# One TensorE program step for scores and PV, and ones columns of the values written by VectorE, in a dilated-attention layer on Trainium2

## The reference, cut to what matters

```
a = rms_norm(x);  [u_pool | q | k | v] = a @ w_in
mixer A: causal means over 2/4/8/16 tokens, minus the token, a 128x128 map per group, a scale
mixer B: 8 heads of 64, q and k normalised per head, T5 bias
  for (window, dilation) in ((128,1), (512,4), (2048,16)):
      blocks of 128 queries against 256 gathered keys (the block before, and the own one)
      p = exp(q k^T + bias), masked;  acc = p @ v;  l = sum(p)
  o = sum of the three acc / sum of the three l
h = x + concat(A, B) @ w_out
y = h + relu(rms_norm(h) @ w_up)^2 @ w_down
```

## Time and profile before

| what | value |
|---|---|
| time, two runs | 2589.89 and 2750.8 us, median 2670.34 us |
| the profiled execution's own time | 2590.12 us |
| its span on the slowest core (core 1) | 2588.6 us |
| spans of the 8 cores | 2569.7 to 2588.6 us |
| PE busy | 2098.6 us (81%) |
| ACT, DVE, POOL busy | 883.8, 850.9, 301.1 us |
| PE's share of the chain that ended last | 67% |

### The profile page before, as it was taken

How to read it: one execution, slowest core, us unless ns; L and a number is a source line. 1 busy time by engine, 2 the same in 40 slices (tenths; PEclk the granted TensorE clock), 3 DMA queues, 4 the chain that set the end, 5 groups by cost and what they waited for, 6 DMA issues and landing times.

```text
span 2588.6 us, 36200 instructions; the slowest of 8 cores (2569.7 to 2588.6 us)
## 1 busy us (share of the span) xinstructions
PE 2098.6 (81%) x11006; PEld 990.3 (38%) x11006; DVE 850.9 (33%) x1197; ACT 883.8 (34%) x1585; POOL 301.1 (12%) x277
## 2 busy tenths in 40 slices
PE   3466667999984999898995677899995989989897
PEld 1222223555541434343332233555552333434342
DVE  0324442444441313222221543344442322223120
ACT  1634615555541312121111454455552312212120
POOL 0001111333330000000000110333330000000000
PEclk8678979555657999999997799656566999999999
DMA  3699981000003646464545332000003445555454
GB/s 68 167 137 164 144 108 21 2 1 2 1 1 85 160 129 172 127 166 130 159 122 157 99 66 33 1 1 1 1 1 81 115 142 159 142 155 143 145 126 128
DMA packets 389896, 243.71 MB, mean 94 GB/s; under 512 B 275104, under 2 KB 368544, under 8 KB 389456
## 3 DMA queue, kind: packets, MB, share of 16 engines
q1 hardware_dynamic: 360080, 198.16, 28.1%
q0 software_dynamic: 29632, 43.24, 12.4%
HBM read 267.77 MB, written 33.60 MB: 116 GB/s over the span
## 4 chain that ended last, share of the span: by engine, by line
PE 67%; DMA 11%; ACT 6%; DVE 6%; issue 6%; POOL 2%; SPq 1%; ACTq 0%; DVEq 0%; POOLq 0%
PE ps L131 64%; ACT abf L139 5%; DMA af<-xc 4%; PE ps L135 3%; DVE af L143 3%; DMA abf<-w_in 2%; DMA abf<-wup_bf 2%; POOL abf L143 1%; DMA abf<-w_out 1%; DVE abf L147 1%; DVE abf L143 1%; ACT af L139 1%; DMA abf<-fd 1%; DMA abf<-xc 1%; SPq L159 1%
## 5 line engine op out<-in xcount | busy, mean ns | idle before, releaser
L131 PE MATMUL ps<-abf 128*128 128x512 bf16 (+2 forms) x4248 | 863.8, 360 | 113.6 <-POOL abf L143 40.8
L131 PE MATMUL ps<-abf,kv 128*128 128x512 bf16 (+1 forms) x3584 | 783.1, 359 | 66.6 <-DVE kv L143 14.5
L131 PEld LDWEIGHTS ps<-abf 128*128 128x128 bf16 (+1 forms) x4248 | 401.2, 111 | 570.0 <-issue 280.1
L139 ACT ACTIVATE abf<-ps 128x512 bf16<-128x512 f32 (+2 forms) x588 | 381.9, 669 | 475.8 <-PE ps L131 266.9
L131 PEld LDWEIGHTS ps<-abf,kv 128*128 128x128 bf16 (+1 forms) x3584 | 332.7, 111 | 437.7 <-issue 231.5
L139 ACT ACTIVATE af<-ps 128x512 f32<-128x512 f32 (+1 forms) x356 | 211.8, 595 | 604.7 <-PE ps L131 603.9
L143 DVE TENSOR_TENSOR kv<-af 128x512 bf16<-128x512 f32 x256 | 177.3, 693 | 303.6 <-ACT af L139 303.6
L143 POOL TENSOR_TENSOR abf<-abf,tabs 128x512 bf16<-128x512 bf16 x192 | 222.0, 1157 | 405.2 <-ACT abf L139 140.7
L131 PE MATMUL ps<-yaT,abf 128*128 128x512 bf16 x672 | 170.7, 406 | 26.5 <-DMA abf<-w_in 13.2
L143 DVE TENSOR_TENSOR abf<-abf,tabs 128x512 bf16<-128x512 bf16 x192 | 84.7, 441 | 308.4 <-ACT abf L139 255.0
L139 ACT ACTIVATE abf<-abf 128x512 f32<-128x512 f32 (+1 forms) x112 | 83.6, 750 | 248.9 <-DVE abf L143 149.0
(11 more groups left out here) (56 smaller groups left out, 888.6 us busy)
## 6 DMA issues: line engine op xcount, KB each, us to landing
abf<-wup_bf SPq DMA_DIRECT2D x256, 256.0 KB, 3.4
abf<-wdn_bf SPq DMA_DIRECT2D x256, 256.0 KB, 2.9
af<-xc SPq DMA_DIRECT2D x64, 512.0 KB, 4.5
abf<-w_in POOLq DMA_DIRECT2D x21, 1024.0 KB, 17.6
abf<-xc SPq DMA_DIRECT2D x16, 512.0 KB, 7.5
wup_bf<-w_up POOLq DMA_DIRECT2D x8, 1024.0 KB, 34.4
wdn_bf<-w_down POOLq DMA_DIRECT2D x8, 1024.0 KB, 39.6
out<-af SPq DMA_DIRECT2D x16, 512.0 KB, 4.7
```

Source lines behind the costliest of these rows:

```text
L131: return lambda e: e.matmul(out, lhsT=lhsT, rhs=rhs, start=start, stop=stop)
L139: return lambda e: e.activation(out=out, in_=in_, func=func, **kw)
```

## The change

Turn i of the loop makes one PE step out of scores(i) and pv(i - 2). The order of the instructions on PE stays: four score matmuls, then four PV matmuls. Their waits now all stand ahead of the first score matmul, and one semaphore increment, at the last PV matmul, stands for both. The steps after them (exp, mult, accumulation) are issued behind it in the order they had. Apart from that the ones columns of vp are written on DVE instead of POOL: a memset instead of the large copy, and the small copies as they were.

```diff
-            P.op("pool", CP(vp[e][:, :, oc:oc + 64], bass.AP(ones64[:].tensor, ones64[:].offset,
-                                                             [list(ones64[:].ap[0]), [0, NVT], [1, 64]])),
-                 reads=[R_const], writes=[R.vp1[e]])
+            P.op("dve", lambda e_, dst=vp[e][:, :, oc:oc + 64]: e_.memset(dst, 1.0), reads=[R_const], writes=[R.vp1[e]])
             if c == 1:
...
-                    P.op("pool", CP(dst, srcb), reads=[R_const], writes=[R.vp1[e]])
+                    P.op("dve", CP(dst, srcb), reads=[R_const], writes=[R.vp1[e]])
...
-        def scores(item):
+        def scores_prep(item):
...
-            P.op("pe", grp(fns), reads=[R_q, R_kv[0], R_kv[1]], writes=[R_bank[sbk]])
             pi = cn["p"] % 3
             cn["p"] += 1
...
+            def post():
+                P.op("act", ACT(PTr[pi], S, AF.Exp), reads=[R_bank[sbk]], writes=[R.PTr[pi]])
+                P.op(eng, TT(PT[pi].rearrange("p (a b) -> p a b", a=2), PTr[pi].rearrange("p (a b) -> p a b", a=2), tab_b, ALU.mult),
+                     reads=[R.PTr[pi], R_tabs], writes=[R.PT[pi]])
+            return (fns, [R_q, R_kv[0], R_kv[1]], [R_bank[sbk]]), post, pi
...
-            P.op("pe", grp(fns), reads=[R.vp[e], R.vp1[e], R.PT[pi]], writes=[R_bank[ob]])
...
+            return (fns, [R.vp[e], R.vp1[e], R.PT[pi]], [R_bank[ob]]), post
...
+            parts, posts = [], []
             if i < NP:
-                pis[i] = scores(pairs[i])
+                part, post, pis[i] = scores_prep(pairs[i])
+                parts.append(part)
+                posts.append(post)
             if i - LOOK >= 0:
-                pv(pairs[i - LOOK], pis.pop(i - LOOK))
+                part, post = pv_prep(pairs[i - LOOK], pis.pop(i - LOOK))
+                parts.append(part)
+                posts.append(post)
+            P.op("pe", grp([f for it in parts for f in it[0]]), reads=[r for it in parts for r in it[1]],
+                 writes=[w for it in parts for w in it[2]])
+            for post in posts:
+                post()
```

More of the change, by code:

```diff
@@ L749, in scores, with pv_prep @@
                     fns.append(MM(S[:, col:col + 128], kvw, qv, start=True, stop=True))
-            P.op("pe", grp(fns), reads=[R_q, R_kv[0], R_kv[1]], writes=[R_bank[sbk]])
             pi = cn["p"] % 3
             cn["p"] += 1
[L753 to L758, removed]
+            eng = "dve" if cn["p"] % 2 == 0 else "pool"
+            def post():
[3 more added lines that the diff above has]
+            return (fns, [R_q, R_kv[0], R_kv[1]], [R_bank[sbk]]), post, pi
+        def pv_prep(item, pi):
             h, p, g4, pr, pair = item
@@ L773, in pv, with post @@
                                   start=(wh == 0), stop=(wh == 1)))
-            P.op("pe", grp(fns), reads=[R.vp[e], R.vp1[e], R.PT[pi]], writes=[R_bank[ob]])
-            if pr == 1:
+            def post():
+                if pr != 1:
+                    return
                 if p == 0:
```

## The result

The changed kernel is slower by 7.1%: the ratio to the kernel before is 1.0712, 95% interval 1.0669 to 1.0756. Its executions took 2762.2 to 2981.45 us, median 2795.34 of 11; the kernel before, over ten, 2583.21 to 2792.11, median 2594.84. The wide ends are executions in which the cores of a die ran at a lower clock; ratio and profiles leave them out. The profiled execution took 2766.1 us against 2590.1, so +176.0 us where the prediction had +160.6. Its slowest core is core 0.

The account below looks back on a forecast made before the run. PE was taken to bound a head, mostly at its low clock. The first head's +11.4, six middle heads' 57.9 and the last's +11.0 gave 80.3 per chunk, 160.6 in all: 2590.1 + 160.6 = 2750.7 us, range 2700 to 2800.

Parts of the forecast that it names:

- The path of one pair: From the matmuls exp waits for, through exp and mult, to the matmuls waiting for mult: 2.47 us on POOL, 1.76 on DVE.
- the sum: One middle head from normalise to normalise, added up by stretches: 49.83 us against 40.18 before, +9.65 per head.
- Both moves on one path: exp released by the last PV matmul and scores(i) waiting for PT(i-2): two-turn period 3.62 us, in dilation 16 4.16.
- the handoff from POOL to PE: Last link of a pair's path, POOL's end to PE's start: 0.25 us, handoffs trusted to 0.1 per period.
- Rival 1, the clock at normalise: Normalise's float32 matmuls may run at the low clock throughout: at most 20 us more, 2770 us; chance 0.17.
- the 9.31: Stretch from normalise's start to step 6, taken to stay at 9.31 us in each middle head.
- Rival 2, a rising clock: Clock rises in attention's thinner PE stream: 76 us less, 2675 us; chance 0.07, including something between.
- Rivals 3 and 4: PT wait at step's head always met, 2548 us; or still at first PV matmul, within 2% of 2590; together 0.06.
- The cost of the boundaries: Boundary between matmul groups on PE, one fewer per turn: saving taken at none, 0.11 us each at most, 2731 us.
- Transposes and columns at nothing: Transposes between steps hide in the gap of about 2.5 us; ones columns on DVE, 11.4 us, finish in time: no cost.

Follow-up runs that it names:

- b4: Changed kernel with all multiplications on DVE instead of every second one on POOL; ratio to the kernel before 1.0233.
- b1: Changed kernel, step still merged, with LOOK = 3 instead of 2; ratio to the kernel before 1.0048.
- Early wait: Changed kernel with two PE steps again, exp released by the scores, but scores(i) also waiting for PT of pair i-2; lowest time 2657.64 us, no ratio.
- late release: Changed kernel with two PE steps again, scores not waiting for PT, but exp waiting for its turn's PV step; ratio to the kernel before 1.0226.
- c1: Changed kernel with only the order of waits ahead of a PE step altered, POOL's last; ratio to the kernel before 1.0536.
- b2: Changed kernel with LOOK = 3 and the two halves of a PV bank tracked as separate resources; ratio to the kernel before 0.9960.
- b3: Changed kernel, LOOK = 2 kept, with the two halves of a PV bank tracked as separate resources; ratio to the kernel before 1.0738.
- a1: Changed kernel with the merge undone, only the ones columns still written by DVE; ratio to the kernel before 0.9984.
- a4: Changed kernel with the step merged but the ones columns back on POOL; ratio to the kernel before 1.0711.
- c2: Changed kernel with LOOK = 3, halved PV banks and normalise in four parts behind turns 3, 5, 7 and 9; ratio to the kernel before 0.9891.
- c3: Kernel before (two PE steps, LOOK = 2) with columns on DVE and normalise in four parts; ratio to the kernel before 0.9927.
- c4: Merged step with LOOK = 3, halved PV banks, normalise in four parts and POOL's wait last; ratio to the kernel before 0.9944.

## Why the prediction was right, point by point

- The direction and the size: 2750 us were forecast, with 2700 to 2800; the profiled execution took 2766.1, the ratio puts it at 7.1% where 6.2% were forecast.
- The path of one pair: shown. Its links are in the trace with their forecast lengths, but for the handoff to PE. Shortening it by POOL's 0.71 us per period (b4) and spreading it over one more turn (b1) both take the loss away by about as much as the sum says.
- Both moves on one path: shown. Early wait and late release alone cost 4.8 and 3.1 us per head, together merged 11.3.
- The term that was mis-sized is the handoff from POOL to PE, 0.25 us taken from a step with one wait behind POOL's, 0.35 measured with two (c1 shows the cause). At some 12 handoffs per head that is 1.2 us, where the sum lacks 1.55 in chunk 1 (51.38 against 49.83) and 1.0 in chunk 2. I had trusted it to 0.1, so the range held it.
- Rival 1, the clock at normalise: not seen. In the head shown, normalise to step 6 took 9.94 instead of 9.31 us, but the 9.31 was the weak reading: among the 14 normalises inside the loop of the kernel before it is the second shortest (9.18 to 10.23, mean 9.77), and I had taken it for all. In the changed kernel the same stretch takes 9.10 to 10.17, mean 9.70. Nor are the float32 matmuls longer: 5.15 to 6.20 us before, mean 5.72; 5.07 to 6.16 after, mean 5.62. So about 0.4 us per head were missing from the sum here, 0.7 in chunk 1, where the short period of 3.17 us behind step 6 in place of 3.62 gave 0.45 of it back. That they partly cancel is luck.
- Rival 2, a rising clock: did not happen, 0.57 per head where it had been 0.59. Rivals 3 and 4: did not happen.
- The cost of the boundaries, taken at none: right. b2 has PE's pace of the kernel before in all three dilations (1.13 and 1.06 in turn for 1.08, 1.11 for 1.11, 1.62 for 1.62 us a pair). The Trainium skill, TensorE: Matmul & The Clock Gate, section The cost: per-tile semaphore tail, prices an increment left out at some 26 ns. No pace here shows such a saving. (What is left out is 190 increments per chunk, 380 in all, where the prediction counted 382.) b2 is 0.4% or 10 us below the kernel before, as the estimate from that page was; but b2 also looks one turn further ahead, so this is not shown to come from it.
- The self-made wait of odd steps was missed. With LOOK = 2 it lies beside the path: b3, which takes it away and has one more wait behind POOL's instead, is no faster. With LOOK = 3 it costs 0.9%.
- Transposes and columns at nothing: right. The columns by a1 and a4; the transposes by dilation 16, where the period from step 20 to 22, which holds transposes, is 4.24 us and that from 22 to 24, which holds none, 4.23. Where the path is shorter (b4) they are paid again.

What stays open: in the head shown three periods are long, where 3.74 (3.70 from 24 to 26) and 4.23 us are usual, each by another handoff. From 10 to 12 it is 4.02, as exp starts 0.48 us after PV's end instead of 0.21; from 24 to 26 it is 3.99, as POOL starts 0.57 us after exp's end instead of 0.26; from 18 to 20 it is 4.37, as PE starts 0.50 us after POOL's end instead of 0.36. In the other heads such periods stand at other steps, at most a few per head. I have no run that tells why.

## What to carry to other kernels

A step is a unit of waiting, not only of work: what is merged starts with the latest of all inputs and releases with the last of all outputs. Before merging two steps of a software pipeline, write down the loop from the merged step's end back to the start of the turn that needs it, and count the turns that stand beside it; if the count falls, raise the lookahead in the same edit. And look at the order in which waits stand ahead of an instruction: put the one that comes last at the end.

## What the runs showed of the hardware that I had not expected

- Waits that have been met are not free when they stand behind the one that was late: PE started 0.14, 0.25, 0.35 and 0.46 us after POOL's end with 0, 1, 2 and 3 of them, and between two orders of the same waits this kernel's time differs by 1.8%.
- A wait of PE for its own step before stretches the start-to-start time from 1.09 to 1.32 us (b1). It asks for the end of the last matmul, about 0.31 us after its start, and PE starts some 0.15 us after that end; without such a wait, in the kernel before, the next group starts about 0.24 us after the start of the last matmul.
- With the float32 matmuls of normalise spread over four turns the granted clock in the attention moved. Its mean over an attention, 0.58 on every core before, was 0.59 to 0.65 in c2 and c3, but 0.54 in chunk 2 on the slowest core of c2, and in c4 0.55 to 0.62. Only that it moved was seen; I varied nothing that would tell why.
